# RWKV recurrence on one core: least distances in the step plan, value copies as four steps, reciprocals of 64 columns

## Reference

```python
def wkv7_scan(s0, r, w, kk, a, k, v):
    def step(s, inp):
        r_t, w_t, kk_t, a_t, k_t, v_t = inp
        s_kk = einsum('bhvk,bhk->bhv', s, kk_t)
        s = (s * w_t[:, :, None, :] - s_kk[..., None] * (kk_t * a_t)[:, :, None, :]
             + v_t[..., None] * k_t[:, :, None, :])
        return s, einsum('bhvk,bhk->bhv', s, r_t)

kk = kk / maximum(sqrt(sum(kk * kk, -1)), 1e-12)        # per head of 64
y: two directions summed, first the 256 context tokens, then the 512 latent tokens
yn = (y - mean) * rsqrt(var + RK_GN_EPS) * lnx_g + lnx_b  # per head of 64
out = ((yn + bonus) * gate) @ w_o
```

## Time and profile before

| | |
|---|---|
| median of 3 runs | 3086.72 us (3081.71, 3086.72, 3093.74) |
| the profiled execution's own time | 3085.09 us |
| its span | 3083.5 us |
| mean granted TensorE clock | 0.978 |
| PE / PEld busy | 2859.8 us (93%) / 2331.1 us (76%) |
| DVE / ACT / POOL busy | 1897.7 (62%) / 1428.7 (46%) / 526.2 (17%) |
| first score of pair 0 starts | 323.6 us |
| last Y of pair 7 | 1012.3 us |

### The profile page before, as it was taken

One profiled execution on the slowest core, in us unless ns is written; L12 is line 12 of the kernel. 1 busy time (PEld: TensorE's weight loads), 2 busy tenths in 40 slices (PEclk: granted clock), 3 DMA queues, 4 the chain that ended last, 5 costly groups with the idle time before them and its releaser, 6 DMA issues. The chain is left out here.

```text
span 3083.5 us, 62817 instructions
## 1 busy us (share of the span) xinstructions
PE 2859.8 (93%) x26751; PEld 2331.1 (76%) x26751; DVE 1897.7 (62%) x3016; ACT 1428.7 (46%) x2197; POOL 526.2 (17%) x482
## 2 busy tenths in 40 slices
PE   7899899998899889999889999999989977999999
PEld 2795677777778658887549999999956744678877
DVE  4941565555665257765778888888864256466652
ACT  1212555655554242221347777777734345343231
POOL 1001545545542010000010000000010045100000
PEclk9999999999999999999999999999989988999999
DMA  5553000000000277655249999999922210222222
GB/s 206 193 191 127 23 21 21 21 21 21 3 3 4 82 255 277 267 198 199 87 153 424 367 369 363 369 367 372 366 99 105 87 36 19 89 77 96 96 96 82
DMA packets 73843, 482.11 MB, mean 156 GB/s; under 512 B 11107, under 2 KB 13027, under 8 KB 32144
## 3 DMA queue, kind: packets, MB, share of 16 engines
q1 hardware_dynamic: 59360, 418.48, 36.0%
q0 software_dynamic: 11952, 51.91, 4.6%
q10 hardware_dynamic: 2304, 8.39, 0.7%
HBM read 457.20 MB, written 34.13 MB: 159 GB/s over the span
## 5 line engine op out<-in xcount | busy, mean ns | idle before, releaser
L2360 DVE TENSOR_TENSOR sb_moe_w_lo<-w_ring,sb_moe_w_hi 128x1408 fp32r<-128x1408 f32 (+1 forms) x132 | 255.3, 1934 | 69.9 <-ACT sb_moe_w_hi L2305 68.3
L2208 PE MATMUL ps<-sb_moe_w_hi,sb_x_feat_lo 128*128 128x352 f32 x832 | 273.4, 329 | 5.2 <-DVE sb_moe_w_lo L2360 5.1
L2210 PE MATMUL ps<-sb_moe_w_hi,sb_x_feat_hi 128*128 128x352 f32 x832 | 267.5, 321 | 0.0
L2209 PE MATMUL ps<-sb_moe_w_lo,sb_x_feat_hi 128*128 128x352 f32 x832 | 266.8, 321 | 0.0
L2305 ACT ACTIVATE sb_moe_w_hi<-w_ring 128x2816 fp32r<-128x2816 f32 x80 | 204.3, 2554 | 2.5 <-DMA w_ring<-w_moe_up 1.8
L2208 PE MATMUL ps<-sb_moe_w_hi,sb_hid_feat_lo 128*128 128x256 f32 x572 | 163.2, 285 | 3.9 <-DVE sb_hid_feat_lo L2491 3.9
L2208 PEld LDWEIGHTS ps<-sb_moe_w_hi,sb_x_feat_lo 128*128 128x128 f32 x832 | 156.1, 188 | 11.5 <-issue 10.4
L2210 PE MATMUL ps<-sb_moe_w_hi,sb_hid_feat_hi 128*128 128x256 f32 x572 | 161.8, 283 | 0.0
L2209 PE MATMUL ps<-sb_moe_w_lo,sb_hid_feat_hi 128*128 128x256 f32 x572 | 161.8, 283 | 0.0
L2209 PEld LDWEIGHTS ps<-sb_moe_w_lo,sb_x_feat_hi 128*128 128x128 f32 x832 | 157.0, 189 | 0.0
L2210 PEld LDWEIGHTS ps<-sb_moe_w_hi,sb_x_feat_hi 128*128 128x128 f32 x832 | 156.0, 187 | 0.0
(11 more groups left out here) (540 smaller groups left out, 7751.2 us busy)
## 6 DMA issues: line engine op xcount, KB each, us to landing
w_ring<-w_moe_up SPq DMA_DIRECT2D x67, 1408.0 KB, 8.4
sb_hm<-w_ada SPq DMA_DIRECT2D x48, 1024.0 KB, 7.1
w_ring<-w_ffn SPq DMA_DIRECT2D x22, 1024.0 KB, 4.9
w_ring<-w_up SPq DMA_DIRECT2D x22, 1024.0 KB, 4.8
sb_b_again<-w_moe_up SPq DMA_DIRECT2D x13, 1408.0 KB, 8.6
sb_hm<-w_moe_up SPq DMA_DIRECT2D x13, 1408.0 KB, 8.2
sb_t_again<-w_moe_up SPq DMA_DIRECT2D x13, 1408.0 KB, 7.7
w_ring<-w_moe_down SPq DMA_DIRECT2D x13, 1408.0 KB, 7.3
```

What stands on the lines that cost most here:

```text
L2208: pe.matmul(out, x_lo, w_hi, start=first, stop=False)
L2209: pe.matmul(out, x_hi, w_lo, start=False, stop=False)
L2210: return pe.matmul(out, x_hi, w_hi, start=False, stop=end)
L2360: return V.tensor_tensor(WL[:, s, w], raw[raw_at(c, i)[0]][:, w], WH[:, s, w].bitcast(F32), ALU.subtract)
```

## The change

A table `behind` sets least distances, in recurrence steps, between a step and the one it waits for: Pmean at least 8 steps behind Gy, Pvar 4 behind the output's Asq, Dbonus 3 behind Pcoef, Pw0 5 behind Dbonus. The spread of pair 0 starts at step 8 and not 4. Av is four steps of the plan, Av0 to Av3, of one copy each. The reciprocals have 64 columns and not 128: twelve for the features, eight for the outputs, each a step of the plan. The waits on `v`, `rec5` and `rec3` become waits on the last piece. All other work is the same; but since the steps are spread evenly and there are now more of them (60 and 18 in place of 51 and 14), nearly every feature and output step lands elsewhere among the recurrence steps.

```diff
-        REC_CUTS = tuple((a, a + P) for a in range(0, TOK, P))
-        OUT_CUTS = tuple((a, a + P) for a in range(0, SEQ, P))
+        REC_CUTS = tuple((a, a + CH) for a in range(0, TOK, CH))
+        OUT_CUTS = tuple((a, a + CH) for a in range(0, SEQ, CH))
...
-                "Drec3", "Drec4", "Drec5", "Dkkn", "APx0", ...
-                "Ag", "Pv", "Av", "GB", "Akd0", ...
+                "Drec3", "Drec4", "Drec5", "Drec6", ... "Drec11", "Dkkn", "APx0", ...
+                "Ag", "Pv", "Av0", "Av1", "Av2", "Av3", "GB", "Akd0", ...
...
-        outs = [... "Aroot", "Drec0", "Drec1", "Drec2", "Drec3", "Gyn", ...
+        outs = [... "Aroot", "Drec0", "Drec1", ... "Drec7", "Gyn", ...
...
+        behind = {"Pmean": ("Gy", 8), "Pvar": ("Asq", 4), "Dbonus": ("Pcoef", 3), "Pw0": ("Dbonus", 5)}
...
-            first, turn, stop = 4, ends[0], len(rec) - 16
-            done = [0, 0]
+            first, turn, stop = 8, ends[0], len(rec) - 16
+            done, at_step = [0, 0], {}
...
-                    while done[at] < len(side) and (done[at] < due and ...
+                    while done[at] < len(side) and i - at_step.get(behind.get(side[done[at]][2], ("", 0))[0], -P) >= behind.get(
+                            side[done[at]][2], ("", 0))[1] and (done[at] < due and ...
                         plan.append(side[done[at]])
+                        at_step[side[done[at]][2]] = i
                         done[at] += 1
...
-                            pool.wait_ge(o_dve.sem, o_dve.at("rec3", p))
+                            pool.wait_ge(o_dve.sem, o_dve.at("rec7", p))
...
-                                act("v", p - 1)
+                                act("v3", p - 1)
...
-                        if x == "v":
+                        if x[0] == "v":
+                            parity, side = divmod(int(x[1]), 2)
                             pe("v")
...
-                            for parity, tokens in enumerate(heads):
-                                for side, hh in enumerate(heads):
-                                    last = S.activation(...)
-                            return last
+                            return S.activation(
+                                VT[heads[side], u, :, :].rearrange(...)[:, :, :, parity, :],
+                                ps[heads[parity], 6:8, 0:3 * P].rearrange(...)[:, :, :, side, :],
+                                ACT.Copy)
...
-                            dve.wait_ge(f_dve.sem, f_dve.at("rec5", p))
+                            dve.wait_ge(f_dve.sem, f_dve.at("rec11", p))
```

More of the change, by code:

```diff
@@ L956, in pairs @@
                 "Asq", "Dscan1.0", "Pnorm", "Dscan1.1", "Aroot", "Dscan1.2", "Gex1", "Drec0", "Gin1", "Drec1", "Drec2",
[2 rows of a table removed]
[2 rows of a table added]
         late = ["Pcoef", "Dbonus"]
-        outs = ["Gy", "Pmean", "Dyc", "Asq", "Pvar", "Aroot", "Drec0", "Drec1", "Drec2", "Drec3", "Gyn", "Aaff", "Gbonus",
+        outs = ["Gy", "Pmean", "Dyc", "Asq", "Pvar", "Aroot", "Drec0", "Drec1", "Drec2", "Drec3", "Drec4", "Drec5", "Drec6", "Drec7", "Gyn", "Aaff", "Gbonus",
                 "Gated"]
@@ L1028, in pairs @@
                         continue
-                    while done[at] < len(side) and (done[at] < due and (side[done[at]][2][0] != "G" or i not in quiet)
+                    while done[at] < len(side) and i - at_step.get(behind.get(side[done[at]][2], ("", 0))[0], -P) >= behind.get(
+                            side[done[at]][2], ("", 0))[1] and (done[at] < due and (side[done[at]][2][0] != "G" or i not in quiet)
                                                     or done[at] and side[done[at]][2] in ("Aw0", "Aw1", "Aa0", "Aa1")
@@ L1297, in feature @@
                             pe.wait_ge(o_act.sem, o_act.at("root", p - 2))
-                        act("v")
+                        act("v3")
                         pe.wait_ge(f_pool.sem, f_pool.at("coefin", p))
@@ L1305, in output @@
                             if p + 2 < N + 1 and p + 1 < N:
-                                pe.wait_ge(f_act.sem, f_act.at("v", p + 1))
+                                pe.wait_ge(f_act.sem, f_act.at("v3", p + 1))
                                 if p + 2 < N:
@@ L1408, in _ @@
                             else:
-                                pe.wait_ge(f_act.sem, f_act.at("v", p))
+                                pe.wait_ge(f_act.sem, f_act.at("v3", p))
                             for d in range(2):
@@ L1500, in feature @@
                                 act.wait_ge(pe_c.sem, pe_c.at(f"Y{NCH - 1}", p - 2))
-                            for parity, tokens in enumerate(heads):
-                                for side, hh in enumerate(heads):
[L1503 to L1506, removed]
-                            return last
+                            return S.activation(
+                                VT[heads[side], u, :, :].rearrange("p (g c q) n -> p g c q n", g=2, c=3, q=2)[:, :, :, parity, :],
+                                ps[heads[parity], 6:8, 0:3 * P].rearrange("p g (c h n) -> p g c h n", c=3, h=2)[:, :, :, side, :],
+                                ACT.Copy)
                         d = int(x[-1])
@@ L1590, in feature @@
                         if x.startswith("rec"):
-                            lo, hi = REC_CUTS[int(x[3])]
+                            lo, hi = REC_CUTS[int(x[3:])]
                             dve.wait_ge(f_act.sem, f_act.at("root", p))
```

## The result

| | before | changed |
|---|---|---|
| median, 15 runs each | 3086.59 us (3081.71 to 3093.74) | 3099.52 us (3092.88 to 3103.82) |
| the profiled execution's own time | 3085.09 us | 3092.88 us |
| GK of one pair to GK of the next | 87.03 us | 88.84 us |

The ratio is 1.0038, 95% interval 1.003 to 1.0046: slower by 0.4%, inside the 0.5% that counts as no change here. The forecast was 3098 us and +2.05 us a pair; measured were 3099.5 us and +1.81 us. The profiled execution of the changed kernel is the fastest of its 15.

The account below looks back on a forecast made before the run. In-order PE was taken to set the pace, a pair changing only with PE's waits. Terms summed to +2.05 us a pair, 12.3 for six, 12.6 with the ends, giving 3098 us; range 3074 to 3112.

Parts of the forecast that it names:

- Root, +1.5: At X4.0: table load and root now run behind W11's copy and delay T3.0's copy; +1.5 us a pair.
- Exponentials, +1.75 and -0.3: At Y4: load and exponentials delay U4's copy, +1.75 us a pair; T4's copies and a moved square give -0.3.
- Pmean, -1.1: At Pmean: Gy comes one score earlier on POOL, so most of the 1.25 us wait goes; -1.1 us a pair.
- Reciprocals, -0.3: On DVE: 1.5 us less waiting at T2.5 and W3, 1.2 new at T2.4, T4.5, T4.6; -0.3 us a pair.
- the split does not halve: Rival on DVE: 64-column pieces cost 0.2 us extra each, 4 us a pair, half on the path; 3110 us, chance 0.04.
- Boundary and value copies, +0.1: Between pairs: Pw0's wait gains 0.5 us, GK 0.6 later behind Akd1 cancels the value copies' gain; +0.1 us a pair.
- Pw0 to Pw1, +0.4: Between Pw0 and Pw1: three T steps instead of seven steps, while Aw0 must finish first; +0.4 us a pair.
- Once each, +0.3: Pair 0's twelve and pair 7's eight bare reciprocals, outside the recurrence: 0 to 1.5 us more, taken as 0.3.
- the waits simply go: Rival: the 5.5 us of PE waits a pair vanish, 33 us over six pairs; 3052 us, chance 0.12.
- the displaced loads cost half: Rival: this, or DVE giving more, takes 1.6 to 2 us a pair off the sum; 3086 to 3089 us, chance 0.18.
- GK held up the first score: Boundary rival: Akd1 2 us later makes GK the bound, each pair starting 1.4 us later; 3106 us, chance 0.14.
- A load did not hold ACT for longer on the path: Denies a rival: each displaced load keeps ACT another 1.28 us, 15 us in all; 3113 us, chance 0.03.

Follow-up runs that it names:

- e1: Changed kernel with the root of kk's norm put back ahead of W11's copy, pairs 1 to 6; 3093.5 us, ratio 1.0021.
- e10: Kernel before with only the table of least distances and the later start of the spread; 3096.2 us, ratio 1.0027.
- e13: Kernel before with the table of distances and later spread start, root kept ahead of W11's copy; 3082.5 us, ratio 0.998.
- e4: Kernel before with only the root moved behind W11's copy, directly ahead of T3.0's, pairs 1 to 6; 3099.3 us, ratio 1.0035.
- e2: Changed kernel with the four exponentials put back to their earlier places; 3085.3 us, ratio 0.9994.
- e6: Changed kernel with the four value copies together again at the last one's place, pairs 1 to 6; 3100.9 us, ratio 1.0044.
- e3: Changed kernel with both the root and the four exponentials put back ahead; 3070.1 us, ratio 0.9943.
- e8: e3 with Akd0 and Akd1 moved ahead of Y5, in front of the value copies, which also come later; 3058.9 us, ratio 0.9902.
- e5: Changed kernel with every other reciprocal taken out and those left doing 128 columns; 3103.3 us, ratio 1.0049.
- e9: e8 with reciprocals re-placed: features' between T4.0 and T0.7, outputs' Drec4 and Drec5 ahead of U2 and T2.5; 3052.4 us, ratio 0.9881.
- e12: Kernel before with only the reciprocals cut to 64 columns, each a step of the plan; 3096.2 us, ratio 1.0031.
- e11: Kernel before with only the value copies Av made four steps of the plan; 3102.9 us, ratio 1.0045.

## Why the prediction was right

The mechanism was right: most of the waits named in the profile went, and two displaced table loads put longer ones in their place. The time was right too (3098 against 3099.5), but in part by luck. The loads cost 3.9 us a pair and not the 2.95 of the sum (1.5 + 1.75 - 0.3), and the rest of the change gave 2.1 and not 0.9; the two errors of about a microsecond cancel. By the first scores the recurrence is 10.9 us longer; the medians say 12.9, and the other 2 us are not traced to a stage. By the steps of the sum:

- **Root, +1.5.** The wait at X4.0 is 1.50 us. Taken back it is worth 2.08 us (e1) or 2.07 (e10 to e13): X4.0 starts 1.67 us later and level 4 behind it takes 0.39 us more, which I had not followed. In the kernel before alone it costs 1.6 (e4).
- **Exponentials, +1.75 and -0.3.** Y4's wait went from 0.69 to 2.50, +1.81; the exchange of -0.3 did not come, since e2 gained 1.83.
- **Pmean, -1.1.** Its row shows no wait any more, and neither does Dyc behind it:

```profile
711.66 1.13 PE L1312 MATMUL ps<-sb_ysum,sb_consts 128*128 128x512 f32 x2
```

- **Reciprocals, -0.3.** T2.5 and W3 waited 1.79 us; now T2.4 and T2.5 wait 0.26 and 0.35, T4.5 and T4.6 0.36 and 0.15, W3 not at all. The 1.5 us gone were as counted, the new waits are 0.77 and not 1.2: this term should have been -0.7. The length of a piece was 0.52 us and not my 0.46. It is near the 0.54 that I had estimated from the fixed part in the Trainium skill (VectorE: DVE Perf Modes, section "The TRN2 errata"). But the overlap decides, 0.43 us from start to start, and of the 1.6 us a pair of more DVE only 0.5 shows. The rival that the split does not halve falls with it.
- **Boundary and value copies, +0.1.** The boundary went as worked out: Pw0 starts 10.0 us after GK's end and T0.0 11.4 (681.82 and 683.28 against 671.86; forecast 9.9 and 11.4), and X0.3 waits 0.50 us for its `first`. So did the margin: the first score waits 0.79 us, and starts when GK, 757.27 + 3.44, is over:

```profile
760.81 0.33 PE L1373 MATMUL ps<-sb_ex_and_FR,sb_sg 64*64 64x64 f32 x4 [0.79 <-issue]
```

e6 gives the value copies' spread 0.2 us net. I had put Akd1's delay at 0.6 us. Gkdk's wait grew from 2.54 to 5.07; in e3, where Y4 does not wait for the load, it is 3.25, so 0.7 us is Akd1's own delay and the other 1.8 is Y4's wait, which holds up PE and ACT while POOL goes on. The two terms together must have been about -0.4 and not +0.1: that is what is left of e3's 2.1 us after Pmean (-1.25), the reciprocals (-0.7) and Aw0 (+0.26).
- **Pw0 to Pw1, +0.4.** PE waits 0.26 us there for Aw0.
- **Once each, +0.3.** The bare reciprocals cost next to nothing: 5.01 and 5.08 us for pair 0's, 3.39 and 3.43 for pair 7's. Pair 0, which I had called even, takes 0.2 us more by its first scores; that its distance from GK to GK went from 77.22 to 78.95 is GK's shift against PE. The profiled recurrence also starts 2.9 us later. Over the profiled executions of all kernels here the first GK starts between 319.8 and 326.4 us, with either length of piece, so I put no cause to this.

Of the rivals, that the waits simply go is refuted for the change as it stands; with the loads put back (e3) the change is faster than the kernel before, by 2.1 us a pair and not the rival's 5.5. That the displaced loads cost half is refuted too: they cost more. That DVE gives more than I took is true in part, 0.4 us a pair. GK held up the first score at its forecast size; e8 shows what the delay of Gkdk behind Akd1 costs in all, 3.3 us a pair in that kernel. A load did not hold ACT for longer on the path either: load, exponential and copies lie end to end.

## What to carry to other kernels

In a plan that spreads steps evenly, the length of a list and the place where the spread starts are knobs: adding steps, or starting later, moves most steps behind it, and the price is set by the few long ones (a table load, a 3.4 us product) that lose their idle stretch. So read the order of every engine at those steps before and after an edit, POOL's too, and pin them to a place (ahead of W11, where ACT stands 3.3 us idle) rather than let a spread find it. And where an engine's long step waits behind short ones of another, as Gkdk behind Akd1, look for the idle stretch that the producer could fill: it gave 3.3 us a pair here, more than the 2.1 of the whole change with its loads put back.

## What the runs showed of the hardware

The granted clock fell to 0.50 for some 3 us behind Y4's wait of 2.50 us in five pairs of e1, five of e5 and two of e6, about 1.5 us each; in the profiled execution of the changed kernel the same wait stands in every pair from 1 to 6 and the clock stayed at 1.00 beside them. In e2, e3, e4, e8, e9, e10, e12 and e13, where no wait of PE in pairs 1 to 6 is over 1.5 us, it never fell beside those pairs; in e11, whose longest is 1.72, it fell in two, behind that wait. Only one execution of each kernel has a trace, and the changed kernel's is its fastest (mean granted clock 0.980, against 0.976 to 0.979 in all but one of the others), so whether the clock fell beside its pairs in the others is open. What PE's pattern ahead of the wait has to do with it was not tried. In these runs a long wait could therefore cost more than its length, and e1's and e5's medians cannot be read without it.
